# Two halves of a weight split, moved in among the normalised high halves of three norms

## The reference

```
h = x                                            # 512 x 1024
layer 0:  u = rms_norm(h) modulated;  h += g1 * even_mixer(u, uc)   # Fourier mixing + neighbourhood attention
          h += g2 * relu(modulate(rms_norm(h)) @ w1)^2 @ w2         # w1 1024x4096, w2 4096x1024
layer 1:  h += g1 * pool_mixer(modulate(rms_norm(h)))
          h += g2 * relu(modulate(rms_norm(h)) @ w1)^2 @ w2
second block: u = rmsnorm(h);  p = u @ w_in + b_in                  # aq, ak, av, hq, hf, hi, hg, gate_a, gate_b
          merged = sigmoid(gate_a) * (sliding-window attention @ w) + sigmoid(gate_b) * (HGRN2 @ w)
          h += merged @ w_out;  u = rmsnorm(h)
          h += (silu(u @ w_gate) * (u @ w_up)) @ w_down
return rmsnorm(h)
```

## Time and profile before

| | |
|---|---|
| median of three runs | 2047.86 us |
| the profiled execution | 2051.87 us |
| its span, first to last instruction | 2050.1 us |
| busy: TensorE | 1994.9 us, 97% |
| busy: VectorE, GpSimd, ScalarE | 960.3, 914.1, 682.7 us |
| mean granted TensorE clock | 0.983 of 2.4 GHz |

### The profile page before, as it was taken

The page is one execution under the profiler, slowest core; times in us unless marked ns, Lnnn a source line. Parts: engine busy times, 40 slices in busy tenths (PEclk is TensorE's granted clock), DMA queues, the critical chain, the costliest instruction groups (busy, mean ns, idle before and its releaser), DMA issues. The chain is left out here.

```text
span 2050.1 us, 25693 instructions
## 1 busy us (share of the span) xinstructions
PE 1994.9 (97%) x10116; PEld 1634.1 (80%) x10116; DVE 960.3 (47%) x1471; ACT 682.7 (33%) x900; POOL 914.1 (45%) x699
## 2 busy tenths in 40 slices
PE   8998998999999999999998999999999999999998
PEld 6875787888888888888887767888888887888887
DVE  4477858583937451413233264266663453113123
ACT  4231733121212431222233354355654342122122
POOL 3323364454545524545454212444344554444444
PEclk9998999999999999999999999999999999999999
DMA  8535132443523312222222111221222222222221
GB/s 349 179 93 213 43 144 109 179 177 147 209 82 148 136 63 99 86 102 95 89 102 89 62 42 59 101 83 62 83 73 92 83 83 103 85 101 103 84 81 42
DMA packets 42783, 223.07 MB, mean 109 GB/s; under 512 B 12737, under 2 KB 13249, under 8 KB 17345
## 3 DMA queue, kind: packets, MB, share of 16 engines
q1 hardware_dynamic: 42688, 221.77, 29.5%
HBM read 217.55 MB, written 2.10 MB: 107 GB/s over the span
## 5 line engine op out<-in xcount | busy, mean ns | idle before, releaser
L970 POOL TENSOR_TENSOR wl<-raw,wh 128x512 fp32r<-128x512 f32 x611 | 833.5, 1395 | 1048.7 <-ACT wh L528 976.3
L1076 PE MATMUL bank<-uh,wh 128*128 128x512 f32 x1432 | 573.9, 401 | 18.4 <-POOL wl L970 17.3
L1078 PE MATMUL bank<-uh,wl 128*128 128x512 f32 x1432 | 560.9, 392 | 0.0
L1077 PE MATMUL bank<-ul,wh 128*128 128x512 f32 x1432 | 560.6, 392 | 0.0
L528 ACT ACTIVATE wh<-raw 128x2048 fp32r<-128x2048 f32 (+1 forms) x152 | 287.0, 1888 | 590.1 <-PE bank L1078 585.6
L1076 PEld LDWEIGHTS bank<-uh,wh 128*128 128x128 f32 x1432 | 270.8, 189 | 87.3 <-POOL wl L970 19.0
L1076 PE MATMUL bank<-ah,wh 128*128 128x512 f32 x848 | 336.2, 396 | 0.0
L1078 PE MATMUL bank<-ah,wl 128*128 128x512 f32 x848 | 334.8, 395 | 0.0
L1077 PE MATMUL bank<-al,wh 128*128 128x512 f32 x848 | 334.7, 395 | 0.0
L1077 PEld LDWEIGHTS bank<-ul,wh 128*128 128x128 f32 x1432 | 270.9, 189 | 57.5 <-issue 3.6
L1078 PEld LDWEIGHTS bank<-uh,wl 128*128 128x128 f32 x1432 | 270.5, 189 | 57.4
(11 more groups left out here) (265 smaller groups left out, 2125.6 us busy)
## 6 DMA issues: line engine op xcount, KB each, us to landing
raw<-in_w SPq DMA_DIRECT2D x64, 1024.0 KB, 5.0
mraw<-in_w_modr SPq DMA_DIRECT2D x32, 1024.0 KB, 4.8
raw<-in_w_gu SPq DMA_DIRECT2D x22, 1024.0 KB, 4.8
raw<-in_w_hg SPq DMA_DIRECT2D x16, 1024.0 KB, 4.9
raw<-in_w_in SPq DMA_DIRECT2D x8, 1024.0 KB, 10.5
modf<-in_w_modf SPq DMA_DIRECT2D x8, 1024.0 KB, 19.7
raw<-in_w_out SPq DMA_DIRECT2D x8, 1024.0 KB, 5.6
mmid<-in_w_modr SPq DMA_DIRECT2D x8, 1024.0 KB, 4.8
```

Source lines behind the costliest of these rows:

```text
L970: last = pool.tensor_tensor(wl[:, b % 2, k:k + 2], raw[:, b % RAW, k:k + 2], f32(wh[:, b % 2, k:k + 2]), ALU.subtract)
L1076: pe.matmul(out, ah_, bh, start=first, stop=False)
L1077: pe.matmul(out, ah_, bl, start=False, stop=False)
L1078: return pe.matmul(out, al_, bh, start=False, stop=last)
```

## The change

The third block of the three norms is no longer split behind the rescale but inside the loop over the highs: its first half ahead of the fifth high (k = 4), its second half ahead of the sixth (k = 5). The split at j = 0 behind the rescale is left out in exchange. The pool norm and the second norm of layer 1 (`mlp1`) are as before.

```diff
+THIRD = {"mlp0": FIRST["mlp0"] + 2, "mix2": FIRST["aq"] + 2, "ffn": FIRST["ffn"] + 2}
...
             def split(b, q=0, per=0, part=None):
 
                 s = b % RAW
+                nk = chunks_of(b, per)
                 if part == 1:
-                    nk = chunks_of(b, per)
                     act.activation(wh[:, b % 2, nk // 2:nk], raw[:, s, nk // 2:nk], ACT.Copy).then_inc(split_hi, 1)
                     return
...
                         split(beside, part=k - 2)
                     if between is not None and k == 6:
                         between()
+                    if name in EARLY and k in (4, 5):
+                        split(THIRD[name], part=k - 4)
                     act.wait_ge(t_ready, 8 * i + k + 1)
...
-                        if not last or j < 7:
+                        if (not last or j < 7) and not (first and j == 0):
                             split(b0 + j + 2, q, 8)
...
-                split(b0 + j + 2)
+                if j:
+                    split(b0 + j + 2)
```

## The result

| | us |
|---|---|
| before, the six runs taken beside it | 2051.64 median (2047.71 to 2052.88) |
| after, six runs | 2032.88 median (2032.33 to 2039.39) |
| ratio after to before | 0.9921, 95% interval 0.9904 to 0.9937 |
| profiled execution: before, after | 2051.87, 2032.75 |
| span: before, after | 2050.1, 2031.0 |

The kernel is 0.8% faster. The forecast was 2033.2, but the sum behind it was 14.7 us, worked from a median of three runs of before (2047.86). Beside its own runs of before the medians differ by 18.8 us, and by 17.0 and 20.3 when both were run again, twice. The ratio in the table is an estimate from all the runs and not the quotient of the two medians: by it the gain is 16.2 us, between 12.9 and 19.7, and in the two repetitions 16.6 (13.5 to 19.7) and 20.9 (17.7 to 24.4).

A forecast was written before the change was run, and what follows sets the result against it. TensorE, busy 97% of the span, bounds the kernel; what is left is mainly its waits for GpSimd's weight lows. Gains of 1.1 + 6.6 + 7.0 = 14.7 us off the 2047.86 median gave 2033.2, range 2028 to 2041.

The forecast's parts named there:

- Which waits go: TensorE's waits for weight lows before blocks 14, 82 and 123 (6.49, 5.13 and 5.51 us) were to vanish.
- The wait moves to block 15: mlp0 norm: block 15's weights, late over SyncE's queue, make TensorE wait 5.3 us there; gain only 1.1 us.
- The half splits: ScalarE, around the fifth high: two half splits of 1.04 us replace one of 1.90, hidden, so GpSimd starts at 325.0.
- Contention: VectorE's last three lows per norm slow beside GpSimd: 0.5 us each in mlp0, 0.95 each in the other two.
- The harsher case that was weighed: Each low pays a whole GpSimd instruction, 1.26 us; last low 0.5 us late in both later norms, sum 1.0 us smaller.
- C: GpSimd slows VectorE's norm more, ending 5 us later in all three; sum 7.2 us, time 2040.7; chance 0.22.
- E: Every VectorE instruction from GpSimd's split on pays one GpSimd instruction, 8.8 us; kernel slower, time 2052.1; chance 0.04.
- The later norms: In the aq and ffn norms the full wait and its slow start go: gains of 6.6 and 7.0 us.
- rival D: The wait reappears in full at blocks 83 and 124; sum 1.1 us, time 2046.8; chance 0.04.
- The slow starts: TensorE at half clock behind the pauses before blocks 14, 82 and 123, costing 1.9, 1.5 and 1.5 us extra.

The follow-up runs named there:

- the reordered load: The changed kernel with the transfer of block 15's weights asked for ahead of modulation block 18 in mlp0: 2032.98 us, ratio to before 0.9905.
- mlp0 alone: The kernel before with the change made in the first of the three norms (mlp0) only: 2049.26 us against 2051.84, ratio 0.9991.

## Why the prediction was right, and where its sum was short

- **Which waits go.** Right: none before 14, 82 and 123, in any of the three profiles.
- **The wait moves to block 15.** Right in mechanism and size: forecast start 350.1 and 5.3 us of waiting, measured 349.52 and 5.03; block 15's end forecast at 363.0, measured 362.41. Gain forecast 1.1, measured 0.75 to 1.96, mean 1.40. The spread is mostly the slow start: charged at 1.9 us, it cost about 1.9, 2.9 and 1.5 in the three profiles (4.0, 6.1 and 3.1 us at half clock, less what its matmuls take at full clock). That the queue was the cause is shown by the reordered load.
- **The half splits.** Right: fitted in, GpSimd starting at 324.71 (forecast 325.0) and ending at 331.1 (331.6 at the latest).
- **Contention.** Direction right. In mlp0 the modulation sum behind the norm begins at 331.81 instead of 330.61; with the 0.15 us by which this execution is ahead that is 1.35 later, where I had charged 1.5. In aq I charged 0.95 a low, 2.9 in all; the rows give 1.25 and 2 x 1.35 instead of 3 x 0.74, 1.7 in all. The harsher case that was weighed, a whole instruction of GpSimd's each time, didn't come, nor did rivals C and E.
- **The later norms.** 6.6 and 7.0 forecast, 6.79 and 7.22 measured. The split of block 83 started as forecast, at 1108.48, or 1111.25 in before's positions against 1111.4. But GpSimd took 5.02 us for it and not the 6.56 charged, and was done at 1115.5, 2.6 us ahead of block 82's end (about 1118.1). So rival D had more than its 1 us of cover against it.
- **The slow starts.** 4.9 charged, 4.7 measured by filling the pauses.
- **What the sum left out.** Norm stages: 1.40 + 6.79 + 7.22 = 15.4, against 14.7. The attention stage: mean 2.1 less in after's three profiles, and nothing was forecast for it. The step of the sum that failed is the silent one, that stages which the change doesn't touch stay as long as they were. In before's two profiles and that of mlp0 alone, the attention stage was within 0.3 us of one value; in the eight with the aq norm changed and the attention's pauses left open it was 0.1 to 2.7 less, in mean 1.8. Seven of these eight lie at 1.05 or more, which speaks for the change. Against it: one of the eight (-0.10) had none of it, and with nothing made earlier and only the pauses of the norms filled the stage was 1.25 less too. So the change neither ensures it nor is needed for it. What is shown is that the clock behind two short pauses makes the difference; how far the change sets that clock, or chance does, stays open. If all of it is counted to the change, 15.4 + 2.1 = 17.5 lies near the 17.0 to 20.3 of the three comparisons; what is left is no more than the start of the program differs by from one execution to the next.
- **The time.** 2033.2 against 2032.88 was helped by chance: the three runs of before from which I subtracted had a median 3.8 us under that of the six.

## What to carry to other kernels

When a wait is removed, look for the transfer that the next block needs, and for whose release it waits: here 5 of one norm's 6.5 us of pause came back one block later, behind one entry in SyncE's queue. A pause of TensorE costs its length and often a stretch at half clock behind it (1.5 to 3.0 us of lost time behind those of 5 us here); price both, and fill the pause with small products where it can't be removed, unless the next stage is bound by another engine. And where GpSimd works beside VectorE, choose what it overlaps: about the same 6.3 us of its work made VectorE 1.35 us later over the lows, and three modulation sums alone 2.7 us longer.

## What the runs showed of the hardware

- Pauses of 1.03 and 1.05 us were followed by half clock in some executions, and pauses of 1.38 and 1.43 us by full clock in others; the pause of 1.08 us before the first scores of after by full clock in its first profile and by half clock in its third; the same 5.13 us pause was followed by slow stretches that differed by 1.56 us in cost. The length of a pause alone didn't tell what came behind.
- A cast of 128x512 on VectorE, with one input, took 1.40 us beside GpSimd's split and 0.43 without; a sum with two inputs 1.66 to 1.78 instead of 0.69. The scalings with an operand in PSUM stayed at 0.75.
